# Column jobs of a hybrid decoder step with their split products ordered by kind, and the wait for the low weights behind the first two kinds

## The reference, cut to what matters

```python
def swiglu(x, wg, wu, wd):
    return (jax.nn.silu(x @ wg) * (x @ wu)) @ wd

def conformer_conv(xn, buf, w_pw1, b_pw1, w_dw, b_dw, ln_g, ln_b, w_pw2, b_pw2):
    a, gate = jnp.split(xn @ w_pw1 + b_pw1, 2, axis=-1)
    h = a * jax.nn.sigmoid(gate)
    ...
    h = causal_dwconv(x_ext, w_dw) + b_dw
    h = jax.nn.silu(layer_norm(h, ln_g, ln_b))
    return h @ w_pw2 + b_pw2, buf_new
```

## Time and profile before

| what | before |
|---|---|
| median of 3 runs | 2718.03 us (2717.55 to 2718.5) |
| the profiled execution's own time | 2717.41 us |
| its span, first to last instruction | 2714.8 us |
| mean granted TensorE clock | 0.996 |
| PE busy | 2658.3 us, 98% |
| PEld busy | 2451.7 us, 90% |
| DVE busy | 1603.1 us, 59% |
| POOL busy | 1348.4 us, 50% |
| ACT busy | 1143.8 us, 42% |
| HBM over the span | 136 GB/s |

### The profile page before, as it was taken

How to read it: one execution, slowest core, us unless ns; L and a number is a source line. 1 busy time by engine, 2 the same in 40 slices (tenths; PEclk the granted TensorE clock), 3 DMA queues, 4 the chain that set the end, 5 groups by cost and what they waited for, 6 DMA issues and landing times.

```text
span 2714.8 us, 44983 instructions
## 1 busy us (share of the span) xinstructions
PE 2658.3 (98%) x16143; PEld 2451.7 (90%) x16143; DVE 1603.1 (59%) x3270; ACT 1143.8 (42%) x1773; POOL 1348.4 (50%) x613
## 2 busy tenths in 40 slices
PE   7999999989989999999999999999999999999999
PEld 5886666679966899999999999999999999999998
DVE  4217768889977343333337885378863788634323
ACT  2217739944423343333333434344344433444433
POOL 0210015610000566667666676676766667666663
PEclk9999999999999999999999999999999999999999
DMA  4320057635574454444454444444445444444453
GB/s 150 98 94 9 16 164 222 200 93 141 153 249 143 124 150 138 136 141 135 139 147 140 134 139 131 140 140 133 140 132 146 133 142 139 132 131 141 148 155 95
DMA packets 457170, 368.87 MB, mean 136 GB/s; under 512 B 15485, under 2 KB 400098, under 8 KB 456716
## 3 DMA queue, kind: packets, MB, share of 16 engines
q1 hardware_dynamic: 444830, 347.05, 43.4%
q0 software_dynamic: 2992, 12.26, 1.5%
q10 hardware_dynamic: 9174, 7.22, 0.9%
HBM read 351.17 MB, written 17.14 MB: 136 GB/s over the span
## 4 chain that ended last, share of the span: by engine, by line
PE 65%; DVE 3%; DMA 1%; ACT 1%; issue 1%; POOL 0%; SPq 0%; ACTq 0%; DVEq 0%
PE bank L2835 20%; PE bank L2837 20%; PE bank L2836 20%; PE bank L2330 4%; DVE bank L3416 1%; DVE tmp L2703 1%; DMA res_b<-park 1%; ACT tmp L2695 1%; PE bank L2710 1%; DMA wring<-in_ffn_w_up 0%; DVE hh L3373 0%; PE bank L3619 0%; DVE hl L3374 0%; PE bank L2350 0%; POOL wl L3294 0%
## 5 line engine op out<-in xcount | busy, mean ns | idle before, releaser
L3294 POOL TENSOR_TENSOR wl<-wring,wh 128x1024 fp32r<-128x1024 f32 x466 | 1139.3, 2463 | 591.9 <-ACT wh L3051 591.7
L2835 PE MATMUL bank<-xh,wh 128*128 128x344 f32 x2688 | 862.2, 321 | 0.0
L2837 PE MATMUL bank<-xh,wl 128*128 128x344 f32 x2688 | 858.4, 319 | 0.0
L2836 PE MATMUL bank<-xl,wh 128*128 128x344 f32 x2688 | 856.8, 319 | 0.0
L3051 ACT ACTIVATE wh<-wring 128x1024 fp32r<-128x1024 f32 x466 | 484.1, 1055 | 764.6 <-PE bank L2837 640.1
L2835 PEld LDWEIGHTS bank<-xh,wh 128*128 128x128 f32 x2688 | 505.6, 188 | 1.5 <-POOL wl L3294 0.3
L2836 PEld LDWEIGHTS bank<-xl,wh 128*128 128x128 f32 x2688 | 504.1, 188 | 1.2
L2837 PEld LDWEIGHTS bank<-xh,wl 128*128 128x128 f32 x2688 | 505.0, 188 | 0.0
L3372 DVE TENSOR_TENSOR bank<-bank,gates_tmp 128x344 f32<-128x344 f32 x132 | 69.1, 524 | 518.1 <-PE bank L2837 424.4
L3416 DVE SCALAR_TENSOR_TENSOR bank<-big,vec,bank 128x344 f32<-128x344 f32 (+1 forms) x696 | 354.7, 573 | 0.5
L2835 PE MATMUL bank<-hh,wh 128*128 128x344 f32 x1040 | 334.4, 322 | 2.7 <-DVE hl L3374 2.7
(11 more groups left out here) (435 smaller groups left out, 3275.9 us busy)
## 6 DMA issues: line engine op xcount, KB each, us to landing
wring<-in_ffn_w_down SPq DMA_DIRECT2D x132, 512.0 KB, 3.5
wring<-in_ffn_w_gate SPq DMA_DIRECT2D x131, 512.0 KB, 3.9
wring<-in_ffn_w_up SPq DMA_DIRECT2D x131, 512.0 KB, 3.9
wring<-in_conv_w_pw SPq DMA_DIRECT2D x72, 512.0 KB, 4.1
big<-in_cache_attn_k SPq DMA_DIRECT2D x128, 256.0 KB, 3.0
big<-in_cache_attn_v SPq DMA_DIRECT2D x128, 256.0 KB, 3.0
wring<-in_w_in SPq DMA_DIRECT2D x20, 512.0 KB, 4.0
park<-res_a SPq DMA_DIRECT2D x1, 4128.0 KB, 11.2
```

Source lines behind the costliest of these rows:

```text
L2835: pe.matmul(bank_out, h, mh, start=(n == 0), stop=False)
L2836: pe.matmul(bank_out, h, ml, start=False, stop=False)
L2837: mm = pe.matmul(bank_out, l, mh, start=False, stop=(n == len(terms) - 1))
L3294: pool.tensor_tensor(wl[s % 6][:, :], raw_w[s % WQ] if raw is None else raw, wh[s % 6][:, :].bitcast(F32), ALU.subtract).then_inc(w_cut, 1)
```

## The change

In `columns_job` the 24 products of a job are now issued by kind: h by xh for all eight tiles, then h by xl for all eight, then l by xh for all eight. Down jobs keep `cut_products`. Ahead of a column job TensorE waits for `wh_done` in place of `w_cut`; the wait for `w_cut` stands between the second kind and the third. `ready(0)` and `ready(1)` stay ahead of tiles 0 and 4 of the first kind, which are now four matmuls apart, not twelve.

```diff
-        def columns_job(pe, J, s, slot, ready=None):
+        def columns_job(pe, J, s, slot, lows=None, ready=None):
             b = s % 6
-            cut_products(pe, job_bank(J), [(wh[b][:, k * P:(k + 1) * P], wl[b][:, k * P:(k + 1) * P],
-                         xh[:, k, chunk(slot)], xl[:, k, chunk(slot)]) for k in range(KD)], ready)
+            h, l = ([w[b][:, k * P:(k + 1) * P] for k in range(KD)] for w in (wh, wl))
+            mh, ml = ([m[:, k, chunk(slot)] for k in range(KD)] for m in (xh, xl))
+            for k in range(KD):
+                if ready and k % HK == 0:
+                    ready(k // HK)
+                pe.matmul(job_bank(J), h[k], mh[k], start=(k == 0), stop=False)
+            for k in range(KD):
+                pe.matmul(job_bank(J), h[k], ml[k], start=False, stop=False)
+            lows()
+            for k in range(KD):
+                mm = pe.matmul(job_bank(J), l[k], mh[k], start=False, stop=(k == KD - 1))
+            mm.then_inc(full, 1)
...
                 for u in range(2):
                     o, uo = (8 + 2 * t + u, 2 + 2 * t + u) if first else (10 * t + u, 4 * t + u)
-                    wait_unit(pe, p, i, uo)
+                    pe.wait_ge(wh_done, lin(i, 6, ATT_UNITS + uoff(p, i) + uo + 1))
                     wait_job_bank(pe, p, i, o)
...
-                    columns_job(pe, off(p, i) + o, uoff(p, i) + uo, SLOT[p], halves_cut(pe, 4 if LAYER[p] else 0, p % 3) if fresh else None)
+                    columns_job(pe, off(p, i) + o, uoff(p, i) + uo, SLOT[p], lambda: wait_unit(pe, p, i, uo), halves_cut(pe, 4 if LAYER[p] else 0, p % 3) if fresh else None)
...
             def pw1(c):
                 for x in range(2 * KD):
                     s, J = PW1_UNIT[c] + x, PW1_JOB[c] + x
-                    pe.wait_ge(w_cut, ATT_UNITS + s + 1)
+                    pe.wait_ge(wh_done, ATT_UNITS + s + 1)
                     pe.wait_ge(free[J % 2], J // 2 + 2)
-                    columns_job(pe, J, s, PW1_SLOT, halves_cut(pe, 1, c) if x == 0 else None)
+                    columns_job(pe, J, s, PW1_SLOT, lambda: pe.wait_ge(w_cut, ATT_UNITS + s + 1), halves_cut(pe, 1, c) if x == 0 else None)
```

More of the change, by code:

```diff
@@ L2909, in pw2 @@
                     s, J = PW2_UNIT[c] + n, PW2_JOB[c] + n
-                    pe.wait_ge(w_cut, ATT_UNITS + s + 1)
+                    pe.wait_ge(wh_done, ATT_UNITS + s + 1)
                     pe.wait_ge(free[J % 2], J // 2 + 2)
-                    columns_job(pe, J, s, CONV_SLOT[c], halves_cut(pe, 2, c) if n == 0 else None)
+                    columns_job(pe, J, s, CONV_SLOT[c], lambda: pe.wait_ge(w_cut, ATT_UNITS + s + 1), halves_cut(pe, 2, c) if n == 0 else None)
             def history(u):
```

## The result

The change makes the kernel slower: 2730.28 us, median of 5 runs (2729.43 to 2733.63), against 2717.92 us. The ratio is 1.005 with a 95% interval of 1.0039 to 1.0061, so 10.6 to 16.6 us; the forecast of 2718.0 us and its range up to 2722.1 us were wrong. The profiled execution of after took 2733.28 us, 3.0 us over its median; its span is 15.8 us longer than that of before.

A forecast was written before the change was run, and what follows sets the result against it. TensorE's matmul stream was taken to bound the late part. Span 2714.8 us, with terms 0 except -0.27 and +0.27, stayed 2714.8; with 2.6 us outside it and the profiled execution 0.6 us under the median: 2718.0 us, range 2715.6 to 2722.1.

The forecast's parts named there:

- The third wait of each job: Added wait between products 16 and 17 of each column job: claimed to cost 0, upper bound 2.0 us for 336 waits.
- a stop at each new wait: Slower rival: TensorE pays 0.10 us (2752 us) or 0.27 us (2809 us) at each of 336 new waits; chance 3%.
- The 0.27 us at the third job: Third column job of the late part: 0.27 us saved on low weights, lost again at the start at 933.79; net 0.
- a wait ahead of the down job that is 0.2 to 0.3 us longer: Sign of being right: TensorE's wait for the low hidden half, before 933.8, grows by what the third job saved.
- The fresh halves: 12 jobs first using newly cut x want its second half 1.26 us earlier: cost 0; slower rival at most 15 us, 1%.
- The order of the 24 products: Issuing each column job's products by kind: claimed change 0, still 156.9 ns a matmul, within 1.6 us either way.
- The stage mean that moved by over 1 ns: Sign of being wrong, in the first pointwise stage: mean start-to-start distance off 156.9 ns, pointing to pairs or alternation.
- pairs with the same weights are cheap today: Slower rival: second load of h saves 13.6 ns today; splitting 2688 pairs costs 37 us, giving 2755 us; chance 2%.
- the 13.6 ns belong to the alternation: Faster rival: runs of one kind free 13.6 ns on 8064 matmuls, 110 us, giving 2608 us (half: 2663); chance 2%.
- 143.3 ns for the columns: Time of 344 columns alone at 2.4 GHz; the remaining 13.6 ns of 156.9 were said to come with every matmul.
- 6% for slower: Summed chance of the three slower rivals, 3%, 2% and 1%; no change had 91%, less than 5.4 us counting as same.

## Why the prediction was wrong, point by point

- **Read right:** TensorE bounds the late part, and its stream is what a change must move. The result shows it: 2 ns a matmul became 14.5 us in the two traces, and 10.6 to 16.6 us in the runs.
- **The third wait of each job, priced at 0:** right. The waits alone measured 1.000 (0.9991 to 1.001), and in the change the distance across the wait has a mean of 158.2 ns, under the 159.0 of all. The rival "a stop at each new wait" (16 ns a wait) is refuted.
- **The 0.27 us at the third job, saved and lost again:** saved, yes. The gap is gone in the run of the waits alone and in the change, whose list of waits of the weight loads no longer has a low weight in it. Lost again is not shown. The sign that the prediction named, a wait ahead of the down job that is 0.2 to 0.3 us longer, is absent: it is 0.52 us with the waits alone, as before, and the time at which that job starts scatters by more than 0.27 us.
- **The fresh halves:** right, no wait for them is in the list of after.
- **The order of the 24 products, priced at 0, bounds of 1.6 us: this step failed.** It said that "today's order contains all steps that could differ". I had sorted the steps by their weights (same h, h to l, l to the next h) and left out the other operand. Sorted by the moving tile, 16 of today's 24 steps stay on the tile number and 8 go on by one; in the new order all go on. The term is 8064 x 2.01 = 16 us in the trace, ten times the bound. The stage mean that moved by over 1 ns (2.1, from 156.9 to 159.0) is one of the prediction's own signs of being wrong, but it gave the sign only to the two rivals below. The bound itself was no bound: it compared two stretches with the tile order (the second has down jobs in it too), and so could only tell how well one reads the mean, not what another order would cost.
- **The rival "pairs with the same weights are cheap today"** had the right sign, 3 times the size (37 us), and the wrong operand: kernels that keep the pairs of h and that break them gave the same 157.89 ns, and one high and one low weight tile used throughout gave the whole loss. The Trainium skill's page "TensorE: Matmul & The Clock Gate" (Part 2, step 1), which the prediction cites here, says that one loads once and multiplies repeatedly. No run tests that: all kernels make 16143 loads for 16143 matmuls, also where the tile stays the same.
- **The rival "the 13.6 ns belong to the alternation"** had the wrong sign. But its premise, that what a matmul takes beyond the prediction's 143.3 ns for the columns can depend on the order, was the right question. I answered it from steps of a timeline in hundredths of a microsecond, in which a mean of 2 ns can't be seen.
- **The chances:** 6% for slower was too little with 8064 repetitions in the stream: 0.67 ns a matmul is already 5.4 us, and no row of the trace excludes 0.67 ns for an order that it doesn't have.

## What to carry to other kernels

When a stream of matmuls is the bound, a reordering is a change to each of them: list for every step what happens to both operands and to the addresses, and give the unknown price of a step that the trace never has at least a nanosecond each way, times the count. Repeating the moving tile (or its twin at the same position in another buffer) before going on to the next was worth 2 ns of 159 here; which sequence is cheap depends on the layout and the width and has to be measured, with the order alone in one kernel and the waits alone in another. The waits that were satisfied long before cost TensorE nothing measurable between two products here (1.000, 0.9991 to 1.001), and gained nothing either.

## What the hardware showed that I had not expected

The distance of matmul starts depends on the sequence in which the moving tiles are used, and by all signs on where they lie: 156.43 to 159.00 ns in the mean for 344 columns with the same weights, loads and counts. The pattern is reproducible: the change, its order alone and the kernel with the weight tiles held have the same mean of 159.00 ns, and kernels of the same sequence agree at every one of the 24 places within about 0.1 ns.

The weights' place seems to take part as well. In the kernel that holds x at tile 0, five of the six weight units lie in one buffer (`big`) and the sixth in another (`wring`). For the middle chunk of tokens the jobs of the five have a mean distance of 155.95 ns and the 13 jobs of the sixth 159.91; for the first chunk it is 157.15 against 156.04, the other way round. With 336 columns and x held there is no such difference (153.3 to 153.5 ns in both). A step of 512 bytes over weight tiles changed nothing, another buffer went with up to 4.0 ns.

And the place is not all. Here is the fourth column job of one round and the same job of the next round, each with the start of the job behind it, in the kernel that holds x. Unit buffer, chunk, moving tile and bank are the same in both:

```profile
2010.16 1.42 PE L2853 MATMUL bank<-xh,wh 128*128 128x344 f32 x8
2013.94 1.42 PE L2853 MATMUL bank<-xh,wh 128*128 128x344 f32 x8
...
2034.56 1.41 PE L2853 MATMUL bank<-xh,wh 128*128 128x344 f32 x8
2038.29 1.41 PE L2853 MATMUL bank<-xh,wh 128*128 128x344 f32 x8
```

The 24 products take 3.78 us in the first and 3.73 us in the second, in the mean 157.8 and 155.5 ns; the round ahead of the two has 155.5 too. The slow stretch is the four jobs behind the product for a mean (line 2940, at 2005.79). So jobs with the same operand addresses have two levels, 2.2 ns apart, and by this stretch what ran before them decides between the two. An account by the addresses within a job can't be the whole one, which fits with sums of steps that don't come out.

The Trainium skill's page "TensorE: Matmul & The Clock Gate" (Part 2, step 1) says that the moving operand and the weight load have two independent read ports, so that loading doesn't steal read bandwidth from the running matmul. From that one would expect the place of the weights not to show in the distance. The trace has up to 4.0 ns between the two buffers, and where the two differ the measurement decides. That the two reads meet somewhere is a guess that fits, not something shown.
